# Padding between the high and the low halves of split fp32 operands in SBUF: low weights 64 bytes further per slot, low activations 192 and low inner values 128 bytes beyond their high halves

## The reference

```python
# block 1: feed-forward, mixer (sliding-window attention + gated linear attention), feed-forward, gated embedding
h = h + 0.5 * swiglu(rmsnorm(h, g1), w_gate, w_up, w_down)      # 1024 -> 2 x 2816 -> 1024
h = h + concat([attn_o, gla_o]) @ w_out                         # from rmsnorm(h) @ w_in
h = h + 0.5 * swiglu(rmsnorm(h, g2), ...)
h = h + sigmoid(rmsnorm(h, g3) @ ple_w_gate) * rmsnorm(p @ ple_w_proj, g4)
# then twice (DEPTH_2 = 2): a mixer, cross-attention into 256 memory tokens, a conv feed-forward
for l in range(2):
    x = x + (even_mixer if l % 2 == 0 else odd_mixer)(rmsnorm(x))
    x = x + mem_attention(rmsnorm(x), rmsnorm(mem), ...)
    x = x + conv_ffn(rmsnorm(x), w_up, w_conv, w_down)
```

## Time and profile before

| what | value |
|---|---|
| median of the two runs | 2561.93 us (2561.89 to 2561.97) |
| span of the profiled execution, first to last instruction | 2561.3 us |
| time of that execution around its span | none recorded; the median is 0.6 us above the span |
| TensorE busy (matmul) | 2541.6 us, 99% |
| VectorE busy | 1596.4 us, 62% |
| ScalarE busy | 912.6 us, 36% |
| matmuls | 12548 |
| share of TensorE in the chain that ended last | 93% |

### The profile page before, as it was taken

How to read it: one execution, slowest core, us unless ns; L and a number is a source line. 1 busy time by engine, 2 the same in 40 slices (tenths; PEclk the granted TensorE clock), 3 DMA queues, 4 the chain that set the end, 5 groups by cost and what they waited for, 6 DMA issues and landing times.

```text
span 2561.3 us, 31974 instructions
## 1 busy us (share of the span) xinstructions
PE 2541.6 (99%) x12548; PEld 2107.0 (82%) x12548; DVE 1596.4 (62%) x1976; ACT 912.6 (36%) x1184; POOL 10.2 (0%) x24
## 2 busy tenths in 40 slices
PE   8999999999999999999999999999999999999999
PEld 7888888778888888877898888888886888888887
DVE  6444468866444468677765747476357665775755
ACT  5222234543222245344443423233146343432322
POOL 0000001000000000000000000000000000000000
PEclk9999999999999999999999999999999999999999
DMA  5222233112222232212321232323210232232222
GB/s 182 102 83 99 96 110 120 67 50 96 103 89 98 99 115 101 99 50 99 132 94 63 104 103 82 115 83 123 94 66 13 87 116 83 84 115 83 101 96 82
DMA packets 37410, 241.91 MB, mean 94 GB/s; under 512 B 4416, under 2 KB 7280, under 8 KB 9136
## 3 DMA queue, kind: packets, MB, share of 16 engines
q1 hardware_dynamic: 34736, 233.78, 26.3%
q10 hardware_dynamic: 1920, 5.22, 0.6%
q0 software_dynamic: 640, 1.31, 0.2%
HBM read 236.89 MB, written 2.10 MB: 93 GB/s over the span
## 4 chain that ended last, share of the span: by engine, by line
PE 93%; DVE 5%; ACT 1%; issue 1%; DMA 0%; POOL 0%; DVEq 0%; ACTq 0%
PE ps L605 24%; PE ps L607 24%; PE ps L606 24%; PE ps L1234 1%; PE ps L623 1%; PE ps L625 1%; PE ps L624 1%; PE ps L766 1%; PE ps L1267 1%; PE ps L1291 1%; PE ps L1282 1%; DVE w_lo L2048 1%; PE ps L768 1%; PE ps L767 1%; PE ps L1303 1%
## 5 line engine op out<-in xcount | busy, mean ns | idle before, releaser
L605 PE MATMUL ps<-op_hi,w_hi 128*128 128x512 f32 x2056 | 800.9, 390 | 0.2 <-DVE op_lo L1929 0.2
L606 PE MATMUL ps<-op_lo,w_hi 128*128 128x512 f32 x2056 | 800.5, 389 | 0.0
L607 PE MATMUL ps<-op_hi,w_lo 128*128 128x512 f32 x2056 | 800.4, 389 | 0.0
L1350 ACT ACTIVATE w_hi<-w_raw 128x2048 fp32r<-128x2048 f32 x217 | 414.4, 1911 | 485.2 <-PE ps L607 315.3
L2048 DVE TENSOR_TENSOR w_lo<-w_raw,w_hi 128x2048 fp32r<-128x2048 f32 x217 | 497.0, 2292 | 38.7 <-ACT w_hi L1350 22.3
L605 PEld LDWEIGHTS ps<-op_hi,w_hi 128*128 128x128 f32 x2056 | 386.3, 188 | 81.4 <-issue 1.4
L607 PEld LDWEIGHTS ps<-op_hi,w_lo 128*128 128x128 f32 x2056 | 386.2, 188 | 80.6
L606 PEld LDWEIGHTS ps<-op_lo,w_hi 128*128 128x128 f32 x2056 | 386.3, 188 | 80.3
L2013 DVE SCALAR_TENSOR_TENSOR x<-ps,x 128x512 f32<-128x512 f32 x134 | 92.7, 691 | 310.8 <-PE ps L607 293.0
L605 PE MATMUL ps<-h_hi,w_hi 128*128 128x512 f32 x692 | 269.5, 389 | 0.0
L606 PE MATMUL ps<-h_lo,w_hi 128*128 128x512 f32 x692 | 269.2, 389 | 0.0
(11 more groups left out here) (373 smaller groups left out, 3085.7 us busy)
## 6 DMA issues: line engine op xcount, KB each, us to landing
w_raw<-in_wstream_dram SPq DMA_DIRECT2D x217, 1024.0 KB, 4.8
cr_m<-in_mem_dram ACTq DMA_DIRECT2D x2, 1024.0 KB, 4.9
w_raw<-in_wstream_dram SPq DMA_DIRECT2D x7, 256.0 KB, 8.0
x<-in_x_dram SPq DMA_DIRECT2D x3, 512.0 KB, 7.3
out_dram<-x SPq DMA_DIRECT2D x3, 512.0 KB, 2.6
m_s<-m_q POOLq DMA_DIRECT2D x16, 64.0 KB, 2.5
ev_s<-in_alibi_dram ACTq DMA_DIRECT2D x1, 1024.0 KB, 4.9
m_c<-in_rope_dram ACTq DMA_DIRECT2D x1, 640.0 KB, 3.9
```

The source lines that it names most:

```text
L605: mm_(o, w_hi[:, c % 4, w], hi[:, k, 0:cols], start=(k == 0), stop=False)
L606: mm_(o, w_hi[:, c % 4, w], lo[:, k, 0:cols], start=False, stop=False)
L607: mm = mm_(o, w_lo[:, c % 4, w], hi[:, k, 0:cols], start=False, stop=(k == kt - 1))
L1350: f_(w_hi[:, c % 4, :], w_raw[:, c % 2, :], ACT.Copy).then_inc(w_hi_ready, 1)
```

## The change

Five unused strips (`fill_...` and the tail of each `w_lo` slot) are put between the tensors, a shared area grows by 512 bytes to hold the wider overlays, and the scratch area for software-made transfers is halved, which frees 8192 bytes per partition. No instruction is added, removed, moved or changed in size: the lists of both programs agree on all five engines, row for row, but for the line numbers.

```diff
-SHARED_BYTES = 32 * 1024
+SHARED_BYTES = 32 * 1024 + 512
         op_hi = sb("op_hi", [P, KT, SEQ], FP32R)
+        sb("fill_op", [P, 48])
         op_lo = sb("op_lo", [P, KT, SEQ], FP32R)
+        sb("fill_w", [P, 80])
         w_hi = sb("w_hi", [P, 4, SLAB], FP32R)
-        w_lo = sb("w_lo", [P, 4, SLAB], FP32R)
+        w_lo = sb("w_lo", [P, 4, SLAB + 16], FP32R)[:, :, 0:SLAB]
+        sb("fill_h", [P, 64])
         with ExitStack() as s:
             h_hi = sb("h_hi", [P, 8, SEQ], FP32R, s)
+            sb("fill_h_lo", [P, 32], FP32, s)
             h_lo = sb("h_lo", [P, 8, SEQ], FP32R, s)
...
-    nc = _bacc.Bacc("TRN2", target_bir_lowering=False, num_devices=1)
+    nc = _bacc.Bacc("TRN2", target_bir_lowering=False, num_devices=1,
+                    dynamic_dma_scratch_size=8192)
```

## The result

The changed kernel takes 2602.01 us (median of two runs, 2601.35 to 2602.68) against 2561.93 before: a ratio of 1.0155, interval 1.0138 to 1.0172. It is 40 us slower, outside the predicted range of 2550 to 2579, though still within the 2% of no change that the prediction gave 0.94.

A forecast was written before the change was run, and what follows sets the result against it. TensorE was taken to bound the kernel, by matmul count times start-to-start distance. All terms were taken as 0 on a 2561.3 us span; with 0.6 us around it, 2561.9 us, range 2550 to 2579.

The forecast's parts named there:

- (a): Everything but `op_lo`, `w_lo` and `h_lo` keeps its remainder by 512, so distances change by whole multiples of 512: cost 0.
- (d): Writes by ScalarE and VectorE into the moved tensors: cost 0; 22 us if the cover of three slots went.
- (e): Halved scratch for GpSimd's transfers: no gain, taken as 0; 11 us if each group waited for one landing more.
- (c): `op_lo` as stationary tile and `w_lo` streamed, in `to_positions` and its like: between -2 and +3 us, taken as 0.
- (b): `op_lo` and `h_lo` streamed at new distances from the loading `w_lo`, 3016 matmuls: bounds 20 and 30 us, taken as 0.
- The one for slower: Unit is 128 bytes, so `op_lo`, streamed from 64 past one, costs 15.4 us: up to 2578 us, chance 0.16.
- The one for faster: Two reads at once clash at equal remainders, new distances relieve it: 2555 us, at most 2532; chance 0.13.

The follow-up runs named there:

- h_same_place: Kernel before with halved scratch, `h_lo` moved by 128 bytes and a 192-byte strip behind `op_lo`, which stays in place: 2568.06 us, ratio 1.0023.
- h_lo_128: Kernel before with halved scratch and only `h_lo` moved, by 128 bytes: 2567.88 us, ratio 1.0022.
- scratch_only: Kernel before with only the scratch halved and the shared area 512 bytes longer, all remainders by 512 kept: 2562.55 us, ratio 1.0001.
- w_lo_step: Kernel before with halved scratch and only the slots of `w_lo` widened, stepping by 64 bytes: 2590.48 us, ratio 1.0111.
- all_32: Kernel before with halved scratch and all six split operands moved by 32 bytes together: 2563.67 us, ratio 1.0007.
- w_both_step: Kernel before with halved scratch, `w_hi` and `w_lo` both stepping by 64 bytes per slot, activations in place: 2593.18 us, ratio 1.0119.
- positions_192: Kernel before with halved scratch, only the nine slabs streamed by `to_positions` and `eighth_positions` 192 bytes further in wider slots: 2560.63 us, ratio 0.9995.
- lo_256: Kernel before with halved scratch, `op_lo` and `h_lo` moved by 256 bytes, `w_lo` at 0, 128, 256, 384 by slot: 2580.24 us, ratio 1.0070.

## Why the prediction was wrong

**What bounds the kernel** was read rightly: TensorE's steps, and nothing else, set the time before and after. But the prediction took 51 us for about what a measurement can tell from no change; the result's interval of 1.0138 to 1.0172 tells 40 us from none clearly.

**Parts (a), (d) and (e)** held. Distances that change by a whole multiple of 512 cost nothing: in `h_same_place` the weights lie 512 bytes further from `op_hi` and `op_lo` than in `h_lo_128`, and the `op` triples step by 226.7 ns in both. The halved scratch costs nothing (`scratch_only`), and the writers take 2292 and 1909 ns per slab, where they took 2292 and 1911.

**Part (c)** was put at 0 within -2 to +3; it came to -2.6 us, just outside. (0.5 us of that stands in the trace of `scratch_only` too, where no distance changed.)

**Part (b) failed**, in two places. The first is the step from the rows to the value 0: "the distances 256 and 512 k are the nearest rows in kind, multiples of 64 both". They were multiples of 256, both, and every tile in the dense stretches is at 0 by 256. The trace of before held no pair at 64, 128 or 192, as I wrote, and the rows 0.23 us apart in the earlier trace rows could say only that 256 is a whole turn. The supporting argument, that a load of 512 bytes runs through every remainder wherever it starts, so that a shift of the start changes nothing, is refuted by slots 1 to 3 of `w_lo_step`, where nothing but the start of `w_lo` is shifted and the step is 231.0 to 231.5 ns. The rows with an offset of 32 were put down to a start off 64; `all_32` shows that they were already the price and the gain of a distance: there the weights lie at the remainder of these tensors, `embeddings` steps by 226.7 ns in place of 233.3, and the first 48 products of the memory's values by 119.8 in place of 116.7. They were the measured sign, in the trace of before, that distances count.

The second is the count. I priced only the matmuls that stream a shifted low activation, 2262 to 3016 of them, at 13.3 and 6.7 ns. `w_lo_step` moves one operand of four, and all three steps of a triple lengthen (in slot 1 to 228.2, 229.0 and 235.8 ns), so that the mean over 9048 is what counts: 3 slots of 4 x 9048 x 4.5 ns = 31 us, less some 2 us given back, for the measured 28. With the right count and the same 6.7 ns at the top, the upper bound of (b) would have been 9048 x 6.7 = 61 us, and 2602 well inside. For `h_lo` alone the prediction's way of counting would have done: there one step of three lengthens, by some 7 ns.

**The rivals.** The one for slower had the wrong unit: at 128, `w_lo` in slot 2 and `h_lo` would be in place, and `h_lo_128` and slot 2 of `w_lo_step` cost. The one for faster was right that the distance between two tiles read at once matters (`w_both_step`), and had the wrong sign for 512 columns; it left out that other distances matter as well. For 256 columns its sign was right: 120.0 became 113.3 or 117.8. What the prediction's last sentence named as what would make it wrong, that a distance moves all three matmuls of a triple, is what happened with `op_lo` and `w_lo`.

**The rule weighed.** By the Trainium skill, "SBUF — State Buffer", section "Who interferes with whom", TensorE's read for streaming and its read for the load have independent ports, and TensorE never waits on anyone. By that every kernel here would take 2562 us; the traces don't agree, with steps from 226.7 to 234.4 ns by nothing but where operands start. The 16-byte lines that the Trainium skill gives on the same page, under Specifications (TRN2), would make offsets of 64, 128 and 192 bytes alike with 0; they aren't.

What stays open: what in SBUF has a period of 256 bytes, and why one set of distances has several rhythms. Most steps that lasted over a slab are near 226.7, 228.9, 230.0, 231.1 or 233.3 ns, so 34 to 35 times 6.67 ns, with thirds and halves of it between. 6.67 ns is the time of 16 columns, by the 226.7 ns for 512 columns and the 120.0 for 256. What stands behind this unit no run here shows. Nor are the tables' means always those of an even step: in slot 3 of `w_lo_step` the triples go through a cycle of four, 689, 702, 700 and 683 ns.

## What to carry to other kernels

When TensorE is the bound and loads a stationary tile for each matmul, look at the distance from start to start and at the remainders by 256 bytes of all operands in the triple: in this kernel all alike gave the shortest step with 512 streamed columns, and the offsets tried that are no multiple of 256 made it up to 3.4% longer. A trace can only exclude what its operands vary in: list the remainders that occur before reading "no effect" out of it. And sizes from one edit don't add to those of another where the engine can stay in a rhythm it came into.

## What the runs showed that was not expected

Several steady rhythms exist at one set of distances: 228.9, 231.1 and 233.3 ns in stretches of `h_same_place`, and 113.3 and 117.8 in the even and the odd mixer's slabs of `positions_192`. One longer step is enough to pass from one to another.

With 256 streamed columns, relations that cost at 512 pay: the 13.3 ns per matmul beyond its columns fell to 6.7 at a distance of 192 bytes, in the even mixer's slabs.

In the trace of the changed kernel, and in that of nine of the twelve others, the granted clock falls to its lower level, 1.2 GHz, once, for a few microseconds, in the odd mixer. Windows of the changed kernel there (busy us and instructions of each engine, then granted clock, DMA share, GB/s):

```profile
1920.00:1923.00 3.00, 1.14 (x10) 1.00 (x8) 2.90 (x4) 2.17 (x3) 0.00 (x0) 1.00 0.00 0
1924.00:1927.00 3.00, 3.00 (x13) 2.19 (x13) 1.36 (x2) 1.39 (x2) 0.00 (x0) 0.50 0.00 0
1928.00:1931.00 3.00, 3.00 (x17) 2.02 (x18) 2.47 (x3) 1.53 (x3) 0.00 (x0) 1.00 0.01 3
```

TensorE was busy for 1.14 us of the 3 before. The steps of the odd mixer's own products (lines 1267, 1282 and 1291 in the kernel before), which run there, sum to 1.1 us more than in the kernel before, whose trace has no such fall: a small part of the 40. The traces of `scratch_only`, `w_lo_step` and `lo_256` have no fall either, so the fall doesn't go with the cost.
